# Down weights in column halves, and a scalar engine whose branch and table load come before the last down copies

## The chip, the cores and the metric

The kernel runs on one core of one Trainium2 chip. The metric is the device time of one execution in microseconds (us). The core has a tensor engine (PE, with its weight loads in rows of their own, PEld), a vector engine (DVE), a scalar engine (ACT), GpSimd (POOL) and a sync engine (SP) that issues nearly all transfers. Each engine runs its own list of instructions in order, and they wait for each other through semaphores.

## The reference

The program is one step of a one-layer decoder for 264 token rows: 256 prompt tokens (16 meta tokens go ahead of them) and 8 decoding sequences. After a mixer (a recurrent branch and a windowed attention) comes a mixture of 32 experts, of which each token takes four, and then a final norm:

```python
logits = (t @ w_router + b_router)
top_v, top_i = lax.top_k(logits, TOP_K)          # 4 of 32 experts a token
...
z = xb @ w_up[e] + b_up[e]                       # 1024 -> 2048
x_glu = jnp.minimum(z[:, ::2], SWIGLU_LIMIT)
x_lin = jnp.clip(z[:, 1::2], -SWIGLU_LIMIT, SWIGLU_LIMIT)
y = x_glu * jax.nn.sigmoid(SWIGLU_ALPHA * x_glu) * (x_lin + 1.0)
return y @ w_down[e] + b_down[e]                 # 1024 -> 1024
...
xp = xp + moe(rmsnorm(xp, norm_ffn), ...)
y_prompt = rmsnorm(xp, norm_final)[:, N_META:]
```

All weights are float32. The experts alone have 32 x (1024 x 2048 + 1024 x 1024) of them, 403 MB, and every one is read once.

## The kernel before

The first 240 us or so are the mixer and the router. Then the experts are computed in 16 pairs (`PAIRS`), two experts side by side, with up to 64 tokens each (`CAP`; a flag says whether an expert has more, and then further rounds run inside an `If`; with this data they do not). A pair's weights come in 12 loads of 2 MB (`PAIR_LOADS`): 8 of `w_up`, 4 of `w_down`. They go through a ring of 8 slots. SP issues each load as soon as the tensor engine has released a slot (semaphore `ring_used`, one count a load). The very last load is issued as two halves of 1 MB, and the second has a semaphore of its own (`half_full`).

For a pair `q` the tensor engine does, in order: the up projection into banks 0 to 3; in between, the combination of the pair before (`combine`, five units, each one 128 x 512 block of the token rows: unit 0 is rows 0 to 127 and columns 0 to 511, unit 1 the same rows and columns 512 to 1023, units 2 and 3 the next 128 rows, unit 4 the tail with both halves); the gather of the next pair's tokens; the transposition of the gated rows `y_e` (`y_rows`, in two halves); and the down projection into banks 4 and 5 (line 1174), bank 4 for output columns 0 to 511 and bank 5 for 512 to 1023. ACT copies the transposed rows to `y_t` (`yt_copy`, line 709, semaphore `yt_ready`) and the two down banks to `yd` (`yd_copy`, line 681, semaphore `yd_ready`). DVE does the gating and adds the combined units to the tokens.

Each of the four down loads of a pair holds two of the eight blocks of 128 rows of `w_down`, and all 1024 columns. So every load feeds both banks, and both banks are complete only with the last load: bank 4 after the first half of it (`down_done`), bank 5 after the second (`ring_used`).

The last pair is different. `y_rows(q, 1)` comes after its first down load, six matmuls without use (`keep_warm`) stand ahead of its down projection, and the five combinations follow the down projection in the order 0, 2, 4, 1, 3 (`LAST_ORDER`), each into a bank of its own. ACT, after its last `yd_copy`, reads the flag (line 739), branches past the `If`, loads the table of the square root with a call on one element (line 748), and goes on to the final norm: a `Square` with a row sum over each 512 columns (line 752, `square`), and three square roots (lines 761, 763, 766), for token rows 0 to 127, for the tail and for rows 128 to 255. DVE adds the units (line 1657), multiplies the first column halves by the norm weights (line 1662), takes the three reciprocals (line 1675) in the order 0, tail, 1 and scales the second column halves (line 1679). ACT scales the first halves (line 770). SP sends the second halves and the tail out (lines 424 to 430), ACT the first halves (line 773).

## Time and profile before

| | |
|---|---|
| median of three runs | 1169.79 us |
| lowest, highest | 1169.16, 1172.5 us |
| the profiled execution | 1169.19 us |
| its span in the trace | 1167.3 us |
| tensor engine busy | 1108.0 us (95%) |
| vector, scalar engine busy | 307.7 us (26%), 228.3 us (20%) |
| mean rate from and to memory over the span | 376 GB/s |

The profile records one execution. Its times are counted from the start of the span, and the span is 1.89 us shorter than the time of the same execution. A busy share is an average over stages with different limits; the rows further down are taken from the stages that matter. The times of matmuls are modelled at their ends, and matmuls overlap, so a group's span is read from its row and not from count times duration.

### The profile page before, as it was taken

The numbers are of one execution on the slowest core, as the hardware profiler recorded it, in microseconds if no ns is written. First come the engines' busy times: TensorE is split into PE (matmuls) and PEld (weight loads), VectorE is DVE, ScalarE is ACT, GpSimd is POOL, SyncE is SP. The second block draws the span as 40 slices with busy tenths as digits, with TensorE's granted clock in tenths as the row PEclk, the third lists the DMA queues.
The fourth block names the chain that finished last, engine by engine and source line by source line (L and its number), as shares of the span: only waits on it lengthen the run. The fifth ranks groups of instructions, "written<-read, shape, count | busy, mean of one in ns | idle before, by whom it ended". The sixth has DMA issues, their size and how long they took to land.

```text
span 1167.3 us, 15067 instructions
## 1 busy us (share of the span) xinstructions
PE 1108.0 (95%) x5796; PEld 501.5 (43%) x5796; DVE 307.7 (26%) x765; ACT 228.3 (20%) x641; POOL 34.0 (3%) x69
## 2 busy tenths in 40 slices
PE   9999999989999999999999898989898999999997
PEld 6687778844343434333332323232333333323322
DVE  6465553032031221313130303030303121203022
ACT  3554363331020202011010101010101010110102
POOL 0200012220000000000000000000000000000000
PEclk9999999999999999999999999999999999999999
DMA  9643637679999999999999999999999999999995
GB/s 359 233 161 108 185 110 289 288 278 411 426 427 429 428 426 427 429 427 428 428 427 429 428 427 429 429 428 428 429 427 429 428 427 429 428 426 428 428 427 202
DMA packets 39375, 438.63 MB, mean 376 GB/s; under 512 B 6576, under 2 KB 8896, under 8 KB 10416
## 3 DMA queue, kind: packets, MB, share of 16 engines
q1 hardware_dynamic: 38568, 436.17, 89.8%
q10 hardware_dynamic: 768, 1.94, 0.4%
q8 instruction: 25, 0.41, 0.1%
q14 instruction: 14, 0.11, 0.0%
HBM read 436.79 MB, written 2.41 MB: 376 GB/s over the span
## 4 chain that ended last, share of the span: by engine, by line
PE 60%; DMA 33%; ACT 3%; DVE 3%; issue 1%; SPq 0%; POOL 0%; ACTq 0%; POOLq 0%
DMA ring<-in_w_up 29%; PE bank L1128 19%; PE bank L1174 15%; PE bank L927 8%; PE bank L972 5%; PE bank L1053 3%; DMA ring<-in_w_down 3%; PE bank L1075 2%; PE bank L1086 1%; ACT area L699 1%; PE bank L1028 1%; DMA ring<-in_w_in 1%; PE bank L1050 1%; PE bank L812 1%; PE bank L1078 0%
## 5 line engine op out<-in xcount | busy, mean ns | idle before, releaser
L1128 PE MATMUL bank<-ring,area 128*64 128x512 f32 x2032 | 462.0, 599 | 30.2 <-DMA ring<-in_w_up 30.2
L1128 PEld LDWEIGHTS bank<-ring,area 128*64 128x64 f32 x2032 | 136.9, 137 | 340.0 <-issue 252.6
L1174 PE MATMUL bank<-ring,area 128*64 128x512 f32 x1008 | 220.4, 594 | 0.5 <-DMA ring<-in_w_down 0.5
L1541 DVE TENSOR_TENSOR x_tok<-x_tok,bank 128x512 f32<-128x512 f32 x60 | 41.3, 688 | 461.9 <-PE bank L1075 461.9
L689 ACT ACTIVATE area<-area 128x256 f32<-128x256 f32 x64 | 26.5, 416 | 550.2 <-DVE area L1553 550.2
L1174 PEld LDWEIGHTS bank<-ring,area 128*64 128x64 f32 x1008 | 71.0, 137 | 141.7 <-issue 135.0
L927 PE MATMUL bank<-ring 128*128 128x264 f32 (+1 forms) x544 | 129.7, 393 | 0.8 <-DMA ring<-in_w_in 0.6
L927 PEld LDWEIGHTS bank<-ring 128*128 128x128 f32 x544 | 101.1, 190 | 24.4 <-issue 4.6
L1075 PE MATMUL bank<-area 128*128 128x512 f32 x128 | 71.5, 643 | 0.0
L681 ACT ACTIVATE area<-bank 128x512 f32<-128x512 f32 x32 | 19.1, 597 | 206.2 <-PE bank L1174 206.2
L972 PE MATMUL bank<-area,ring 128*128 128x264 f32 x256 | 58.7, 388 | 0.0
L1053 PE MATMUL bank<-area,h_tok 128*128 128x128 bf16 x768 | 53.1, 220 | 0.0
L972 PEld LDWEIGHTS bank<-area,ring 128*128 128x128 f32 x256 | 48.1, 190 | 8.0 <-issue 0.2
L1053 PEld LDWEIGHTS bank<-area,h_tok 128*128 128x128 bf16 x768 | 49.5, 98 | 0.0
L1553 DVE TENSOR_SCALAR area<-bank 128x256 f32<-128x256 f32 x64 | 26.9, 420 | 76.0 <-PE bank L1128 75.9
L1075 PEld LDWEIGHTS bank<-area 128*128 128x128 f32 x128 | 19.2, 188 | 51.3 <-issue 51.3
L699 ACT ACTIVATE area<-bank,vec 128x128 f32<-128x128 f32 x120 | 34.3, 368 | 20.5 <-PE bank L1053 20.5
L1086 PE MATMUL bank<-keep,area 128*128 128x128 f32 x128 | 17.7, 280 | 13.7 <-ACT area L699 13.7
L1578 DVE TENSOR_TENSOR area<-area 128x1024 f32<-128x1024 f32 x15 | 18.4, 1225 | 40.4 <-ACT area L699 40.4
L1050 PE MATMUL bank<-area,h_tail 72*128 72x128 bf16 x128 | 28.5, 223 | 0.0
L1557 DVE SCALAR_TENSOR_TENSOR area<-area 128x256 f32<-128x256 f32 x64 | 27.2, 425 | 2.2
L1028 PE MATMUL bank<-bias_parts,chosen 96*128 96x512 bf16 x96 | 26.7, 388 | 0.5 <-ACT area L705 0.5
(252 smaller groups left out, 622.7 us busy)
## 6 DMA issues: line engine op xcount, KB each, us to landing
ring<-in_w_up SPq DMA_DIRECT2D x127, 2048.0 KB, 31.6
ring<-in_w_down SPq DMA_DIRECT2D x55, 2048.0 KB, 34.8
ring<-in_w_in SPq DMA_DIRECT2D x17, 1024.0 KB, 7.7
ring<-in_w_down SPq DMA_DIRECT2D x16, 1024.0 KB, 32.9
ring<-in_w_out SPq DMA_DIRECT2D x8, 1024.0 KB, 4.9
area<-in_w_up SPq DMA_DIRECT2D x1, 2048.0 KB, 26.8
area<-in_w_down SPq DMA_DIRECT2D x1, 2048.0 KB, 7.6
ring<-in_x_cols SPq DMA_DIRECT2D x2, 560.0 KB, 4.5
```

The source lines that it names most:

```text
L699: ins = act(xe[:, j, :], bank[6 + half][:, P * i:P * (i + 1)], ACT.Copy, scale=vec[:, NFF + j:NFF + j + 1])
L927: m = mm(proj_bank(n)[:, 0:T - lo], w[:, k, P * (n % 2):P * (n % 2) + P], (xn if n < 2 else h_t)[:, k, lo:T], start=(k == 0), stop=(k == K ...
L972: mo = mm(bank[m % 2][:, 0:NT], w[:, k, :], m_t[:, k, N_META:T], start=(k == 0), stop=(k == 2 * KB - 1))
L1028: mm(bank[b0 + n - n0][:, :], chosen[:, :], bias_parts[:, NB * n:NB * (n + 1)], start=True, stop=False, skip_group_check=True)
L1050: mm(out, h_tail[0:TRIO, P * j:P * (j + 1)], g_oh[0:TRIO, 2, :], start=True, stop=False)
L1053: m = mm(out, parts[:, t, i, P * j:P * (j + 1)], g_oh[:, t, :], start=False, stop=(t == 1 and i == 2))
L1075: m = mm(b[:, :], gw_t[:, lo:lo + P], yd[:, NB * c:NB * (c + 1)], start=True, stop=True)
L1086: tr = eng.transpose(bank[6 + half][:, P * i:P * (i + 1)], y_e[:, P * (4 * half + i):P * (4 * half + i + 1)], ident)
L1128: m = mm(bank[2 * h + n][64 * e:64 * e + 64, :], xe[:, k, 64 * e:64 * e + 64], w[:, kk, e, NB * n:NB * (n + 1)], start=False, stop=(k == K ...
L1174: m = mm(bank[4 + c][64 * e:64 * e + 64, :], y_t[:, f, 64 * e:64 * e + 64], w[:, c, e, j, :], start=False, stop=(f == KB - 1), skip_group_ ...
L1541: eng.tensor_tensor(x, x, combined_bank(unit, last)[:, :], ALU.add).then_inc(s.added, 1)
L1557: eng.scalar_tensor_tensor(out=lin[:, n % 2, :], in0=lin[:, n % 2, :], scalar=1.0, in1=glu[:, n % 2, :], op0=ALU.add, op1=ALU.mult).then_i ...
```

## The change

Three things change. First, the host packs `w_down` differently and the tensor engine reads it so: a load holds four blocks of rows and one half of the output columns. Loads 0 and 1 complete bank 4, loads 2 and 3 complete bank 5. In the last pair, `combine(q, 0)` follows load 1, and the others follow load 3. Both `yd_copy` calls now wait for `ring_used`. Second, in ACT's program `yd_copy` of the last pair moves behind the reading of the flag and the `If`, and the call that loads the square root's table moves ahead of the flag; a first `square` stands between the two last copies. Third, the square root and the reciprocal of the tail come last, the half sums come earlier, and the stores follow that order; ACT issues each of its two stores right behind the scaling that it belongs to.

The lists of the two compiled programs show what stands where. Scalar engine, end of the program before; `area` is the working memory (here `yd`), `bank` a PSUM bank:

```order
L689 ACTIVATE area<-area 128x256 [waits y_ready,glu_ready] x2
L709 ACTIVATE area<-bank 128x512 [waits ytr_done]
L681 ACTIVATE area<-bank 128x512 [waits down_done,combine_done]
L681 ACTIVATE area<-bank 128x512 [waits ring_used]
L739 TENSOR_LOAD flag
L739 ISA x2
```

and, past the `If`:

```order
L748 ACT_TABLE_LOAD
L748 ACTIVATE stat<-eps 128x1
L752 ACTIVATE area,stat<-x_tok 128x512 [waits final_added] x2
L752 ACTIVATE area,stat<-x_tail 72x512 [waits final_added]
L752 ACTIVATE area,stat<-x_tok 128x512 [waits final_added]
L761 ACTIVATE stat<-stat 128x1 [waits squares,sumsq]
L763 ACTIVATE stat<-stat,eps 72x1 [waits sumsq]
L752 ACTIVATE area,stat<-x_tok 128x512 [waits final_added]
```

Scalar engine, the same places of the changed program (its lines 678, 706, 743, 759 and 771 are lines 681, 709, 748, 752 and 761 of before):

```order
L686 ACTIVATE area<-area 128x256 [waits y_ready,glu_ready] x2
L706 ACTIVATE area<-bank 128x512 [waits ytr_done]
L743 ACT_TABLE_LOAD
L743 ACTIVATE stat<-eps 128x1
L744 TENSOR_LOAD flag
L744 ISA x2
```

and, past the `If`:

```order
L678 ACT_TABLE_LOAD [waits ring_used]
L678 ACTIVATE area<-bank 128x512 [waits combine_done]
L759 ACTIVATE area,stat<-x_tok 128x512 [waits final_added]
L678 ACTIVATE area<-bank 128x512 [waits ring_used]
L759 ACTIVATE area,stat<-x_tok 128x512 [waits final_added]
L759 ACTIVATE area,stat<-x_tail 72x512 [waits final_added]
L759 ACTIVATE area,stat<-x_tok 128x512 [waits final_added]
L771 ACT_TABLE_LOAD [waits squares]
L771 ACTIVATE stat<-stat 128x1 [waits sumsq]
L759 ACTIVATE area,stat<-x_tok 128x512 [waits final_added]
```

The last two copies of the down banks moved behind the branch. One table load stood there, ahead of everything; now three stand in the program: one ahead of the branch, one at the first copy behind it and one at the first square root.

Tensor engine, the down projection of the last pair and what follows it, before:

```order
L1174 MATMUL bank<-ring,area 64x512 [waits ring_full6,yt_ready]
L1174 MATMUL bank<-ring,area 64x512 x7
L1086 MATMUL bank<-keep,area 128x128 [waits y_ready]
L1086 MATMUL bank<-keep,area 128x128 x3
L1174 MATMUL bank<-ring,area 64x512 [waits ring_full7]
L1174 MATMUL bank<-ring,area 64x512 x7
L1174 MATMUL bank<-ring,area 64x512 [waits ring_full0,yt_ready]
L1174 MATMUL bank<-ring,area 64x512 x7
L1174 MATMUL bank<-ring,area 64x512 [waits ring_full1]
```

and changed (lines 1180, 1093 and 1082 are 1174, 1086 and 1075 of before):

```order
L1180 MATMUL bank<-ring,area 64x512 [waits ring_full6,yt_ready]
L1180 MATMUL bank<-ring,area 64x512 x7
L1093 MATMUL bank<-keep,area 128x128 [waits y_ready]
L1093 MATMUL bank<-keep,area 128x128 x3
L1180 MATMUL bank<-ring,area 64x512 [waits ring_full7,yt_ready]
L1180 MATMUL bank<-ring,area 64x512 x7
L1082 MATMUL bank<-area 128x512 [waits yd_ready,gwt_ready]
L1180 MATMUL bank<-ring,area 64x512 [waits ring_full0]
L1180 MATMUL bank<-ring,area 64x512 x7
L1180 MATMUL bank<-ring,area 64x512 [waits ring_full1]
```

The second wait for `yt_ready` moved from the third load to the second, and `combine(q, 0)`, with its wait for the copied bank, now stands between the second load and the third.

The diff:

```diff
--- before.py
+++ after.py
@@ -144,7 +144,7 @@
 x_biased x_negmax x_sink_exp x_exp x_scaled ga_sig attn_gated wout_used final_added x2_ready
 split_copy split_sub h2_tr logits_done negtop top_exp selb_ready rank_done flag_ready cast_ready gather_oh weight_oh
 gather_done xt_ready up_done glu_ready lin_ready sig_ready gated_ready y_ready ytr_done yt_ready gwt_tr
-gwt_ready down_done yd_ready combine_done added ring_used window_stored 
+gwt_ready yd_ready combine_done added ring_used window_stored 
 y_final stored router_step lru_step x_step
 """.split()
 
@@ -423,11 +423,11 @@
             eng.wait_ge(s.y_final, 3)
             eng.dma_start(y_prompt[0, 0:P, NB:D], h_tok[:, 0, NB:D]).then_inc(s.stored, 16)
             eng.wait_ge(s.y_final, 4)
+            eng.dma_start(y_prompt[0, P:2 * P, NB:D], h_tok[:, 1, NB:D]).then_inc(s.stored, 16)
+            eng.wait_ge(s.y_final, 5)
             for half in range(2):
                 eng.dma_start(y_sample[:, 0, NB * half:NB * (half + 1)], h_tok[64 * half:64 * half + B_S, 2, 0:NB])\
                    .then_inc(s.stored, 16)
-            eng.wait_ge(s.y_final, 5)
-            eng.dma_start(y_prompt[0, P:2 * P, NB:D], h_tok[:, 1, NB:D]).then_inc(s.stored, 16)
 
             eng.wait_ge(s.stored, 16 * (5 + 6))
             eng.wait_ge(s.window_stored, 16 * 10)
@@ -670,15 +670,12 @@
                 act(ex[0:n, t, :], lg[0:n, t, 0:E_N], ACT.Exp, bias=ntop[0:n, t:t + 1]).then_inc(s.top_exp, 1)
 
 
-            def yd_copy(q):
-
-                eng.wait_ge(s.combine_done, 5 * q)
-                for c in range(2):
-                    if c == 0:
-                        eng.wait_ge(s.down_done, q + 1)
-                    else:
-                        eng.wait_ge(s.ring_used, PAIR_LOADS * q + PAIR_LOADS)
-                    act(yd[:, NB * c:NB * (c + 1)], bank[4 + c][:, :], ACT.Copy).then_inc(s.yd_ready, 1)
+            def yd_copy(q, c):
+
+                if c == 0:
+                    eng.wait_ge(s.combine_done, 5 * q)
+                eng.wait_ge(s.ring_used, PAIR_LOADS * q + (UP_LOADS + 2 * c + 2))
+                act(yd[:, NB * c:NB * (c + 1)], bank[4 + c][:, :], ACT.Copy).then_inc(s.yd_ready, 1)
 
             def sigmoid(q, n):
                 eng.wait_ge(s.glu_ready, 4 * q + (n + 1))
@@ -726,49 +723,59 @@
                     gwt_copy(q)
                     yt_copy(q, 0)
                 yt_copy(q, 1)
-                yd_copy(q)
 
             rrow_copy(0)
+            def yd_copies(q):
+                yd_copy(q, 0)
+                yd_copy(q, 1)
+
             pair(0, True)
+            yd_copies(0)
             pair(1, True)
+            yd_copies(1)
             with eng.Fori(1, PAIRS // 2 - 1) as it:
-                pair(2 * it, True)
-                pair(2 * it + 1, True)
+                for u in range(2):
+                    pair(2 * it + u, True)
+                    yd_copies(2 * it + u)
             pair(PAIRS - 2, True)
+            yd_copies(PAIRS - 2)
             pair(PAIRS - 1, False, True)
+            act(stat[:, 14:15], eps[:, :], ACT.Sqrt)
             more = eng.value_load(flag[0:1, 0:1], min_val=0, max_val=1)
             with eng.If(more > 0):
                 with eng.Fori(PAIRS // 2, PAIRS // 2 * ROUNDS) as it:
                     for u in range(2):
+                        yd_copies(2 * it + u - 1)
                         rrow_copy(2 * it + u)
                         xe_copy(2 * it + u, 0)
                         xe_copy(2 * it + u, 1)
                         pair(2 * it + u, False)
 
-            act(stat[:, 14:15], eps[:, :], ACT.Sqrt)
+                eng.wait_ge(s.combine_done, 5 * (PAIRS * ROUNDS - 1))
+                eng.wait_ge(s.ring_used, PAIR_LOADS * PAIRS * ROUNDS)
 
             def square(step, x, n, col):
                 eng.wait_ge(s.final_added, step + 1)
                 act(junk[0:n, NB * step:NB * (step + 1)], x, ACT.Square, accum_out=stat[0:n, col:col + 1])\
                     .then_inc(s.squares, 1)
 
+            yd_copy(PAIRS - 1, 0)
             square(0, x_tok[:, 0, 0:NB], P, 0)
+            yd_copy(PAIRS - 1, 1)
             square(1, x_tok[:, 1, 0:NB], P, 1)
             square(2, x_tail[0:TRIO, :], TRIO, 2)
-            square(3, x_tok[:, 0, NB:D], P, 3)
-            eng.wait_ge(s.sumsq, 2)
-            eng.wait_ge(s.squares, 3 * KB + 4)
-            act(stat[:, 6:7], stat[:, 3:4], ACT.Sqrt, bias=stat[:, 5:6], scale=1.0 / D).then_inc(s.root, 1)
+            for t in range(2):
+                square(3 + t, x_tok[:, t, NB:D], P, 3 + t)
+                eng.wait_ge(s.sumsq, 2 + t)
+                eng.wait_ge(s.squares, 3 * KB + 4 + t)
+                act(stat[:, 6 + t:7 + t], stat[:, 3 + t:4 + t], ACT.Sqrt, bias=stat[:, (5, 15)[t]:(6, 16)[t]],
+                    scale=1.0 / D).then_inc(s.root, 1)
             eng.wait_ge(s.sumsq, 6)
             act(stat[0:TRIO, 8:9], stat[0:TRIO, 2:3], ACT.Sqrt, bias=eps[0:TRIO, :], scale=1.0 / D).then_inc(s.root, 1)
-            square(4, x_tok[:, 1, NB:D], P, 4)
-            eng.wait_ge(s.squares, 3 * KB + 5)
-            act(stat[:, 7:8], stat[:, 4:5], ACT.Sqrt, bias=stat[:, 15:16], scale=1.0 / D).then_inc(s.root, 1)
             for t in range(2):
                 eng.wait_ge(s.y_final, t + 1)
-                eng.wait_ge(s.rstd_ready, 2 * t + 2)
+                eng.wait_ge(s.rstd_ready, t + 2)
                 act(h_tok[:, t, 0:NB], h_tok[:, t, 0:NB], ACT.Copy, scale=stat[:, 9 + t:10 + t]).then_inc(s.y_scaled, 1)
-            for t in range(2):
                 eng.wait_ge(s.y_scaled, t + 1)
                 eng.dma_start(y_prompt[0, P * t:P * (t + 1), 0:NB], h_tok[:, t, 0:NB]).then_inc(s.stored, 16)
 
@@ -1161,24 +1168,22 @@
                 biases(4, 6, 4)
                 if last:
                     keep_warm(6, bank[0])
-                for fp in range(KB // 2):
-                    if fp % 2 == 0:
-                        eng.wait_ge(s.yt_ready, 2 * q + (fp // 2 + 1))
-                    w = full(u, UP_LOADS + fp, it).rearrange("p (c e j n) -> p c e j n", c=2, e=2, j=2)
-                    for c in range(2):
-                        if u == 1 and fp == KB // 2 - 1 and c == 1:
+                for i in range(4):
+                    c, half = divmod(i, 2)
+                    if c == 0:
+                        eng.wait_ge(s.yt_ready, 2 * q + (half + 1))
+                    w = full(u, UP_LOADS + i, it).rearrange("p (f e n) -> p f e n", f=4, e=2)
+                    for f in range(4):
+                        if u == 1 and i == 3 and f == 2:
                             eng.wait_ge(s.half_full, 16 * it + 16)
-                        for j in range(2):
-                            for e in range(2):
-                                f = 2 * fp + j
-                                m = mm(bank[4 + c][64 * e:64 * e + 64, :], y_t[:, f, 64 * e:64 * e + 64],
-                                       w[:, c, e, j, :], start=False, stop=(f == KB - 1), skip_group_check=True)
-                                if j == 1 and c == 1 and e == 1:
-                                    m.then_inc(s.ring_used, 1)
-                                elif f == KB - 1 and e == 1:
-                                    m.then_inc(s.down_done, 1)
-                    if last and fp == 0:
+                        for e in range(2):
+                            m = mm(bank[4 + c][64 * e:64 * e + 64, :], y_t[:, 4 * half + f, 64 * e:64 * e + 64],
+                                   w[:, f, e, :], start=False, stop=(half == 1 and f == 3), skip_group_check=True)
+                    m.then_inc(s.ring_used, 1)
+                    if last and i == 0:
                         y_rows(q, 1)
+                    elif last and i == 1:
+                        combine(q, 0, True)
 
             pair(0, 0, 0, 0, True, first=True)
             pair(1, 1, 0, 1, True)
@@ -1188,7 +1193,7 @@
             pair(PAIRS - 2, 0, PAIRS // 2 - 1, PAIRS - 2, True)
             pair(PAIRS - 1, 1, PAIRS // 2 - 1, PAIRS - 1, True, last=True)
 
-            for unit in LAST_ORDER:
+            for unit in LAST_ORDER[1:]:
                 combine(PAIRS - 1, unit, True)
 
             eng.wait_ge(s.flag_ready, 1)
@@ -1656,10 +1661,10 @@
                 x = x_tok[:, t, cols] if unit < 4 else x_tail[:, :]
                 eng.tensor_tensor(x, x, combined_bank(unit, True)[:, :], ALU.add).then_inc(s.final_added, 1)
                 if step < 2:
-                    if step == 1:
-                        half_sum(0)
                     eng.wait_ge(s.final_added, step + 1)
                     eng.tensor_tensor(h_tok[:, t, cols], x, norm_b[:, cols], ALU.mult).then_inc(s.y_final, 1)
+                    if step == 0:
+                        half_sum(0)
                 elif step == 2:
                     half_sum(1)
                 elif step == 3:
@@ -1669,11 +1674,11 @@
                     eng.wait_ge(s.sumsq, 5)
                     eng.tensor_tensor(stat[0:TRIO, 2:3], stat[0:TRIO, 2:3], rr[0:TRIO, 0:1], ALU.add).then_inc(s.sumsq, 1)
 
-            for step, t in enumerate((0, 2, 1)):
+            for t in range(3):
                 n = height[t]
-                eng.wait_ge(s.root, step + 3)
+                eng.wait_ge(s.root, t + 3)
                 eng.reciprocal(stat[0:n, 9 + t:10 + t], stat[0:n, 6 + t:7 + t]).then_inc(s.rstd_ready, 1)
-                eng.wait_ge(s.rstd_ready, step + 2)
+                eng.wait_ge(s.rstd_ready, t + 2)
                 out, x, scale = ((h_tok[0:n, 2, 0:NB], x_tail[0:n, :], norm_t[0:n, :]) if t == 2
                                  else (h_tok[:, t, NB:D], x_tok[:, t, NB:D], norm_b[:, NB:D]))
                 eng.scalar_tensor_tensor(out=out, in0=x, scalar=stat[0:n, 9 + t:10 + t], in1=scale,
@@ -1703,7 +1708,7 @@
     if name == "w_up":
         return a[0].reshape(PAIRS, 2, 4, 2, P, 2, D).transpose(0, 5, 2, 4, 3, 1, 6).reshape(PAIRS, KB, P, SLOT)
     if name == "w_down":
-        return a[0].reshape(PAIRS, 2, KB // 2, 2, P, 2, NB).transpose(0, 2, 4, 5, 1, 3, 6).reshape(PAIRS, KB // 2, P, SLOT)
+        return a[0].reshape(PAIRS, 2, 2, 4, P, 2, NB).transpose(0, 5, 2, 4, 3, 1, 6).reshape(PAIRS, KB // 2, P, SLOT)
     return a
```

## Rows read from the trace of the kernel before

**Rows 1.** The page: rate of the transfers in 40 equal slices of the span.

```profile
GB/s 359 233 161 108 185 110 289 288 278 411 426 427 429 428 426 427 429 427 428 428 427 429 428 427 429 429 428 428 429 427 429 428 427 429 428 426 428 428 427 202
```

**Rows 2.** Chain that ended last, near its end: start, duration, what.

```profile
1111.63 35.62 DMA ring<-in_w_down
...
1147.39 7.10 PE bank L1174 x32
```

**Rows 3.** Stretches: length, busy time by engine, clock, DMA share, GB/s.

```profile
1151.50:1154.50 3.00, 3.00 (x15) 0.93 (x11) 0.00 (x0) 0.60 (x1) 0.00 (x0) 1.00 0.00 0
```

**Rows 4.** Timeline, last down projection on PE and ACT: start, duration, what.

```profile
1143.26 3.65 PE L1174 MATMUL bank<-ring,area 128*64 128x512 f32 x16
1143.36 0.60 ACT L709 ACTIVATE area<-bank 128x512 f32<-128x512 f32 x1 [5.57 <-PE bank L1086]
...
1154.40 1.98 PE L1075 MATMUL bank<-area 128*128 128x512 f32 x4
1154.51 0.60 ACT L681 ACTIVATE area<-bank 128x512 f32<-128x512 f32 x1 [1.06 <-PE bank L1174]
...
1155.81 1.28 ACT L748 ACT_TABLE_LOAD   x1 [0.70 <-issue]
...
1157.11 0.20 ACT L748 ACTIVATE stat<-eps 128x1 f32<-128x1 f32 x1
```

**Rows 5.** Timeline, the same places of the pair before the last but one.

```profile
1022.80 1.09 ACT L709 ACTIVATE area<-bank 128x512 f32<-128x512 f32 x2 [0.54 <-PE bank L1086]
...
1023.56 13.95 PE L1174 MATMUL bank<-ring,area 128*64 128x512 f32 x64
```

**Rows 6.** Timeline of DVE, ACT and PE after the last down projection.

```profile
1155.67 0.69 DVE L1657 TENSOR_TENSOR x_tok<-x_tok,bank 128x512 f32<-128x512 f32 x1 [17.23 <-PE bank L1075]
...
1156.32 1.08 PE L1078 MATMUL bank<-area 128*64 128x512 f32 x4
...
1157.33 1.99 PE L1075 MATMUL bank<-area 128*128 128x512 f32 x4
...
1158.62 0.68 DVE L1657 TENSOR_TENSOR x_tail<-x_tail,bank 128x512 f32<-128x512 f32 x1
...
1159.34 0.63 ACT L752 ACTIVATE area<-x_tail 72x512 f32<-72x512 f32 x1 [0.80 <-DVE x_tail L1657]
...
1160.09 0.14 DVE L1667 COPY rr<-stat 8x1 f32<-8x1 f32 x1
...
1160.52 0.68 DVE L1657 TENSOR_TENSOR x_tok<-x_tok,bank 128x512 f32<-128x512 f32 x1
...
1160.81 0.29 ACT L761 ACTIVATE stat<-stat 128x1 f32<-128x1 f32 x1
1161.23 0.63 ACT L752 ACTIVATE area<-x_tok 128x512 f32<-128x512 f32 x1
...
1161.99 0.29 ACT L766 ACTIVATE stat<-stat 128x1 f32<-128x1 f32 x1
```

**Rows 7.** The same timeline, last scaling and two of the stores.

```profile
1162.12 0.37 SPq L424 DMA_DIRECT2D out_y_prompt<-h_tok  x1
...
1163.11 0.72 ACT L770 ACTIVATE h_tok<-h_tok,stat 128x512 f32<-128x512 f32 x1 [0.21 <-DVE stat L1675]
...
1163.83 0.36 SPq L430 DMA_DIRECT2D out_y_prompt<-h_tok  x1
```

**Rows 8.** Stretches of the stores, columns as in rows 3.

```profile
1162.50:1163.00 0.50, 0.00 (x0) 0.00 (x0) 0.50 (x2) 0.40 (x1) 0.00 (x0) 1.00 0.07 25
1163.50:1166.25 2.75, 0.00 (x0) 0.00 (x0) 0.30 (x1) 0.33 (x1) 0.00 (x0) 0.51 0.90 315
```

**Rows 9.** Timeline, tensor engine behind two waits for a load.

```profile
1013.49 3.65 PE L1128 MATMUL bank<-ring,area 128*64 128x512 f32 x16 [1.24 <-DMA ring<-in_w_up]
...
1044.21 5.28 PE L1128 MATMUL bank<-ring,area 128*64 128x512 f32 x16 [2.14 <-DMA ring<-in_w_up]
```

**Rows 10.** The stretch behind the longer wait, columns as in rows 3.

```profile
1044.20:1047.60 3.40, 3.39 (x8) 1.01 (x10) 0.00 (x0) 0.00 (x0) 0.00 (x0) 0.51 0.99 419
```

## The prediction, written before the changed kernel had run

> **What bounds the kernel now.** I first read the page's rates by slice [rows 1]: from the tenth slice to the last but one the core moves 411 to 429 GB/s without a dip, although the tensor engine is busy all the while. For most of the program the stream of expert weights sets the pace. The chain of waits says the same near the end [rows 2]: a down load is issued at 1111.63 us, travels for 35.62 us behind the loads before it, and on landing releases 32 matmuls. Then I read the stretches [rows 3]: from 1151.5 us on nothing is moved at all. So the stream ends there, and what follows, some 16 us, is a chain of dependent work. Nothing in the change touches the number, size or order of the weight transfers, so I expect everything up to about 1143 us where it is, and the question is only the tail. I read that from the timeline: the reader should see PE without a gap from 1147.39 to 1159.3 us [rows 2, 4, 6], and behind it DVE and ACT handing small work to each other.
>
> **The steady state.** A down load still releases its slot after eight matmuls. The second load now needs the second half of `y_t`, where before the third did. In a pair inside the loop both copies are done at 1022.80 + 1.09 = 1023.89 us, and the second load starts a quarter into the 13.95 us that begin at 1023.56, at about 1027.0 [rows 5]. The work on the first load hides the wait with 3 us to spare, so it costs nothing. The earlier copy of bank 4 meets an idle ACT and nobody asks for it before the next pair. Zero for the 15 pairs.
>
> **The second load of the last pair.** Here `y_rows(q, 1)` stands behind the first load. Before, the second load started at 1143.26 us and the copy of the transposed half ran beside it, from 1143.36 for 0.60 us [rows 4]. Now the second load waits for that copy: 1143.36 + 0.60 + 0.05 = 1144.01, which is 0.75 later. It takes 3.65 and ends at 1147.66.
>
> **The combination ahead of the third load.** PE works through its list in order. `combine(q, 0)` now stands ahead of the third load and waits for the copy of bank 4. That copy starts when the second load ends, and the list of ACT shows that a table load stands ahead of it and carries the wait for `ring_used`. So the load isn't hidden in ACT's idle time: 1147.69 + 1.28 + 0.02, copy 0.60, and PE gets its bank at 1149.64. Both durations are rows [rows 4]. PE idles for 1.98 us. The unit itself takes 0.96 (two in the 1.92 from 1154.40 to 1156.32 [rows 4, 6]) to 1.05; I take 1.0. The third load starts at 1150.65, where it started at 1147.39 [rows 2]. Everything has landed by 1151.5, so the 16 + 16 matmuls run through as before in 7.01 us (1147.39 to 1154.40) and the next unit starts at 1157.66, that is **+3.26**.
>
> **Four units instead of five.** Unit 2 needs only bank 4's copy, and unit 4 gets bank 5's during it (copy of 0.60). 0.96 + 1.01 later, at 1159.63, units 1 and 3 start, before at 1157.33 [rows 6]: the unit taken out is worth **-0.96**, and the difference is +2.30.
>
> **DVE.** A unit's add starts 1.27 us after the unit (1154.40 to 1155.67 [rows 4, 6]). Before, DVE was late for unit 1, since it had to do four adds and products first. Now one add and product are done early. The tail's add comes at about 1160.25, and unit 1's at 1160.92, bound by PE, where it was at 1159.29 (0.67 behind the tail's add at 1158.62, a step I keep). That gives back **-0.67**: +1.63.
>
> **The second table load.** `square` starts 0.72 after the add (1158.62 to 1159.34), the root 0.76 after the square (1161.23 to 1161.99) [rows 6]. So the third-last square starts at 1161.64, and at 1162.40 comes what was not there: the list shows a table load between it and the first root, **+1.28** and 0.02. The root runs at 1163.70, before at 1160.81: +2.89. The load is there because ACT can reach this place from the `If` with another table in place; the load ahead of the branch is therefore not enough, and the first copy behind the branch asks for one table and the root for another. The last square follows at 1163.92, the last of the two prompt roots at 1164.68, before at 1161.99: the tail's root, now last, gives back **-0.20**, +2.69.
>
> **What is removed.** The read of the flag and the branch (0.70 idle) and a table load (1.28) stood behind the last copy [rows 4]. They held back only the first square, which has DVE's work beside it. Now they run in ACT's idle time before 1147.66: 1143.96 + 1.28 + 0.20 + about 0.8 is 1146.2. That is free, but what it frees wasn't the end of the chain: units 4, 1 and 3 on PE ran until 1159.32 anyway.
>
> **The stores.** From 1164.68 ACT does the tail's root (0.20), the first scaling (0.70), an issue (0.36), the second scaling (0.72) and an issue (0.36), which with the small gaps ends at 1167.30; before, the last issue began at 1163.83 and ended at 1164.19 [rows 7]. That is +0.4 over the shift. In return only one store is late. A store issued at 1162.12 was seen moving only around 1163.0 [rows 7, 8], and before three of them had to go at once, at 315 GB/s until 1166.25, with 1.05 from there to the end of the span at 1167.3. Now the last 256 KB start at 1166.94 + 0.85 and take 0.83 at that rate, or up to 1.3 behind the store ahead: 1168.6 to 1169.1, and with 1.05 the span ends at 1169.7 to 1170.2. I take 1170.0.
>
> **The sum.** +3.26 - 0.96 - 0.67 + 1.28 - 0.20 is +2.71 at the roots, and the stores leave it: span 1167.3 + 2.7 = 1170.0. The same execution took 1.89 more than its span, so 1171.9. The profiled execution (1169.19) lies 0.6 under the median, and another may lie either side; I say 1172.2, which is +2.4 us or 0.2%. About 0.3%, 3.5 us, is what a measurement of this kernel can tell from no change, so this falls within it, on the slow side.
>
> **Bounds of what no row shows.** The table load that carries a wait: if it started before its wait were met, its 1.28 would be hidden, PE's gap would be 0.7 and the time 1170.7 to 1170.9; at the other end it costs all of its 1.28, as the only one in the tail did. I take the full cost, since the list is explicit. The order of banks in the matmuls changes (16 records to one bank in place of 8): the loads with the old order take 3.65 for 16 in every stage, and I take the same; nothing else in the rows bears on it.
>
> **Rivals.**
> *The clock falls in the new gap* (slower by over 0.3%). PE waited 1.24 us for a load once a pair, and the 16 matmuls behind it took 3.65 as always; once it waited 2.14, and they took 5.28 [rows 9], with a granted clock of 0.51, that is 1.2 GHz, over the following 3.4 us [rows 10]. My gap of 1.98 lies between the two and near the longer. If the clock falls there, the matmuls of the third load take 1.63 longer, and since all weights have landed nothing absorbs it: 1173.6 to 1173.9, +0.33% to +0.35%. It decides from the point at which a gap is long enough, somewhere from 1.24 to 2.14; whether it falls may differ between executions. Chance 0.38.
> *The first table load is hidden* (above): 1170.8, chance 0.10.
> *The stream covers it* (the side of faster). If the third load landed only at about 1150.6, the combination would use time that PE waits anyway. The end of the down projection would not move: 1171.9 - 3.26 = 1168.7, a gain of 0.1%. Rows 2 and 3 speak against it: it landed at 1147.25 and all was quiet at 1151.5. Chance 0.04. Even with the second table load gone as well (-1.28) that is 1167.4; a gain of 3.5 us is in no case, and I leave 0.04 for what the trace doesn't show.
> *A table switch costs more than its row.* ACT's row of the load is 1.28, and the next ACTIVATE starts 0.02 behind its end, at 1157.11 [rows 4]. If something of the same size stood beside each of the two loads on the path, the time would be 1171.9 + 2.6 = 1174.5. Chance 0.03. The Trainium skill says this: "ScalarE: Activation LUTs", section "What ACT_TABLE_LOAD costs", gives about 1283 ns for the load, which the trace confirms, and some 1380 ns more for a drain with every change of set, which the row here does not show; by it the sum would be about 1174.7.
>
> **Chances and range.** The forecast as worked out has 0.41, the clock 0.38, the hidden load 0.10, the drain 0.03, covered 0.04, unknown gain 0.04. My sum may be off by 0.7 us, so a part of the first case lands beyond 3.5 us and a part of the clock's case below it. Slower by over 0.3%: 0.44. Within 0.3%: 0.51. Faster: 0.05. The likeliest case alone spans 1171.2 to 1173.2. The range goes down to the hidden load, 1170.2, and up to the clock's case with its error, 1174.8.
>
> **What would show it.** Right: a gap of about 2 us on PE ahead of the first combination, filled by a table load and a copy on ACT; the last four units starting around 1157.7; a table load of 1.28 between the last squares and the first root, at about 1162.4; weights still all landed by 1151.5. Wrong: a PE gap of 0.7 or less; the third load's matmuls in 5.3 us; no load at the root; or any difference before 1143 us, in the rate of the stream above all.

## The result and the profile after

The changed kernel took 1174.41 us (median of 9 runs, 1172.18 to 1177.21), the kernel before 1169.75 us (9 runs, 1168.91 to 1172.5). The ratio is 1.0040, with a 95% interval of 1.0031 to 1.0048: slower by 4.7 us, or 0.4%, and clear of noise. That is within the stated range. It is not the case that I called likeliest (1172.2, within 0.3% of no change) but the one that I gave 0.38, in which the clock falls in the new gap.

The execution that was profiled took 1176.95 us, with a span of 1175.2. It began its last down projection 2.90 us later than the one before, at 1141.98 us in place of 1139.08, for a reason that has nothing to do with the tail (below). Times in the tail are therefore compared from that start on. The timeline of the changed kernel, PE and ACT in the last down projection, with start, duration and what, and in brackets the idle time before and its releaser, answers to [rows 4]:

```profile
1141.98 3.65 PE L1180 MATMUL bank<-ring,area 128*64 128x512 f32 x16
...
1146.26 0.60 ACT L706 ACTIVATE area<-bank 128x512 f32<-128x512 f32 x1 [5.57 <-PE bank L1093]
1146.88 1.28 ACT L743 ACT_TABLE_LOAD   x1
1146.91 3.66 PE L1180 MATMUL bank<-ring,area 128*64 128x512 f32 x16 [0.69 <-ACT area L706]
...
1150.66 1.28 ACT L678 ACT_TABLE_LOAD   x1 [2.29 <-PE bank L1180]
1151.96 0.60 ACT L678 ACTIVATE area<-bank 128x512 f32<-128x512 f32 x1
1152.70 1.10 PE L1082 MATMUL bank<-area 128*128 128x512 f32 x2 [2.13 <-ACT area L678]
1153.72 8.78 PE L1180 MATMUL bank<-ring,area 128*64 128x512 f32 x32
...
1162.44 1.13 PE L1082 MATMUL bank<-area 128*128 128x512 f32 x2
```

The reader should see the chain of the prediction step by step: the second load waits 0.69 for the copy of `y_t`; when it ends, ACT loads a table (1.28), only then copies (0.60), and PE has stood still for 2.13 us when it takes up the combination. The 32 records behind it take 8.78 us, where they took 7.10 [rows 2]. The stretches show why (length, busy time of PE, PEld, DVE, ACT and POOL, clock, DMA share, GB/s):

```profile
1150.60:1152.70 2.10, 0.00 (x1) 0.03 (x1) 0.00 (x0) 1.88 (x2) 0.00 (x0) 1.00 0.79 324
1152.70:1154.30 1.60, 1.60 (x4) 0.46 (x6) 0.37 (x1) 0.00 (x0) 0.00 (x0) 0.90 0.30 123
1154.30:1157.70 3.40, 3.40 (x12) 1.06 (x10) 1.16 (x3) 0.72 (x2) 0.00 (x0) 0.55 0.01 2
1157.70:1162.40 4.70, 4.70 (x24) 1.36 (x20) 0.00 (x0) 0.00 (x0) 0.00 (x0) 1.00 0.01 3
```

The fall comes a little over 1 us behind the gap: over the first 1.6 us the granted clock is 0.90, then PE worked for 3.4 us at a granted 0.55, nearly all at 1.2 GHz, and then at 2.4 GHz again. By 1154.30, which is 1151.40 in the times of before, the weights have landed, as forecast. The end of the program, answering to [rows 6, 7]:

```profile
1165.67 0.69 DVE L1662 TENSOR_TENSOR x_tok<-x_tok,bank 128x512 f32<-128x512 f32 x1
...
1167.19 1.28 ACT L771 ACT_TABLE_LOAD   x1
1168.48 0.29 ACT L771 ACTIVATE stat<-stat 128x1 f32<-128x1 f32 x1
...
1169.48 0.29 ACT L771 ACTIVATE stat<-stat 128x1 f32<-128x1 f32 x1
...
1170.61 0.36 ACTq L780 DMA_DIRECT2D out_y_prompt<-h_tok  x1
...
1171.07 0.72 ACT L778 ACTIVATE h_tok<-h_tok,stat 128x512 f32<-128x512 f32 x1 [0.49 <-DVE stat L1680]
...
1171.82 0.34 ACTq L780 DMA_DIRECT2D out_y_prompt<-h_tok  x1
```

The second table load stands between the last square but one and the first root, as the list of instructions said. At the very end an issue of 0.36 stands between the two scalings.

Counted from the first down load, each milestone of before and after (the last column is the difference):

| from the first down load, us | before | after | shift |
|---|---|---|---|
| second load starts | 4.18 | 4.93 | +0.75 |
| third load starts | 8.31 | 11.74 | +3.43 |
| next unit after the down projection | 15.32 | 20.46 | +5.14 |
| DVE adds unit 1 | 20.21 | 23.69 | +3.48 |
| first root | 21.73 | 26.50 | +4.77 |
| last root of the prompt rows | 22.91 | 27.50 | +4.59 |
| ACT's last issue of a store ends | 25.13 | 30.18 | +5.05 |
| end of the span | 28.22 | 33.22 | +5.00 |

### The profile page after: what moved, and what is told of

The parts are those of the page before. It is cut to its first block, busy times and chain, and to the rows that moved or that the text cites. A ratio compares the mean times of both kernels' runs of the same rounds, so it can differ in the third digit from the quotient of the medians.

```text
span 1175.2 us, 15074 instructions
## 1 busy us (share of the span) xinstructions
PE 1110.0 (94%) x5794; PEld 503.1 (43%) x5796; DVE 308.1 (26%) x765; ACT 230.8 (20%) x643; POOL 33.9 (3%) x69
## 3 DMA queue, kind: packets, MB, share of 16 engines
q10 hardware_dynamic: 768, 1.94, 0.5%
## 4 chain that ended last, share of the span: by engine, by line
PE 63%; DMA 30%; ACT 4%; DVE 2%; issue 1%; SPq 0%; POOL 0%; ACTq 0%; POOLq 0%
DMA ring<-in_w_up 29%; PE bank L1180 19%; PE bank L1135 17%; PE bank L934 8%; PE bank L979 5%; PE bank L1060 4%; PE bank L1082 2%; PE bank L1093 1%; ACT area L696 1%; PE bank L1035 1%; PE bank L1057 1%; DMA ring<-in_w_in 1%; PE bank L819 1%; PE bank L1045 0%; PE bank L810 0%
```

## The experiments

Each kernel was timed in five rounds against the kernel before. Beside each median stands the ratio with its 95% interval. "Last root" is the last prompt root, counted from the first down load in the profiled execution; it is 22.91 before the change and 27.50 after it. The kernel before, timed beside each group, had medians of 1169.56 to 1169.86.

**The combination behind the last load.** `combine(q, 0)` goes back behind the last load, and with it ACT's two copies stand side by side; both table loads are kept:

```diff
             yd_copy(PAIRS - 1, 0)
+            yd_copy(PAIRS - 1, 1)
             square(0, x_tok[:, 0, 0:NB], P, 0)
-            yd_copy(PAIRS - 1, 1)
...
-                    elif last and i == 1:
-                        combine(q, 0, True)
...
-            for unit in LAST_ORDER[1:]:
+            for unit in LAST_ORDER:
```

> The changed kernel with combine(q, 0) moved back behind the last down load, and ACT's two last copies next to each other ahead of the first square (otherwise the square would wait for a unit that comes later). Both table loads stay. Theory (the gap of 2.1 us in front of the first combination costs 3.3 us of the tensor engine's order and the lower clock 1.7 us on top): no gap, the third load's matmuls start 0.3 us later than before the change and take 3.6 us each at full clock; the first table load is hidden, the second stays on the path with 1.28 us; time 1171.0 +- 0.7. Rival (the place of the combination does not matter, the two table loads make all the difference): 1173.5 or more.

Measured: 1171.22 us, ratio 1.0014 (1.0005 to 1.0023), last root at 23.97, +1.06. The timeline shows 48 records in one piece and the first table load beside them:

```profile
1143.71 10.52 PE L1180 MATMUL bank<-ring,area 128*64 128x512 f32 x48 [0.69 <-ACT area L706]
...
1147.47 1.28 ACT L678 ACT_TABLE_LOAD   x1 [2.29 <-PE bank L1180]
...
1160.46 1.28 ACT L771 ACT_TABLE_LOAD   x1
```

With the combination in its old place 3.2 us of the 4.7 are gone. The table loads alone cannot be the cause of these, since both are still there; the first one costs only where PE stands behind it.

**Work without use in the gap.** The gap stays as long as it is, but PE is busy in it:

```diff
                     elif last and i == 1:
+                        keep_warm(8, bank[1])
                         combine(q, 0, True)
```

> The changed kernel with eight matmuls without use (128x512, bf16, into bank 1, some 1.7 to 2.1 us) in the gap in front of the first combination. Theory (the granted clock falls because of the gap): the clock stays at 1.0 through the third and fourth down load, the 32 records take 7.1 us in place of 8.8, the unit starts where it did or 0.1 later; time 1172.7 +- 0.6, and the spread between runs shrinks. Rival (the clock falls for another reason, or costs nothing that counts): 1174.4 as the changed kernel, or more by the added matmuls.

Measured: 1172.66 us, ratio 1.0023 (1.0014 to 1.0032), runs from 1171.99 to 1173.82, last root at 25.80. The unit starts as late as ever, and the matmuls behind it run at full clock, as the stretch shows:

```profile
1147.31 1.91 PE L790 MATMUL bank<-ones 128*128 128x512 bf16 x8
...
1149.51 1.10 PE L1082 MATMUL bank<-area 128*128 128x512 f32 x2 [0.29 <-ACT area L678]
1150.54 7.09 PE L1180 MATMUL bank<-ring,area 128*64 128x512 f32 x32
```

```profile
1150.60:1157.50 6.90, 6.90 (x33) 2.14 (x32) 1.53 (x3) 0.72 (x2) 0.00 (x0) 1.00 0.03 10
```

So 1.75 us of the changed kernel's time is the clock, bought back by useless matmuls (1.70 at the last root), and the gap itself still costs its length.

**No table load behind the branch.** One square root on one element more, at the end of the `If`:

```diff
                 eng.wait_ge(s.ring_used, PAIR_LOADS * PAIRS * ROUNDS)
+                act(stat[:, 14:15], eps[:, :], ACT.Sqrt)
```

> The changed kernel with one more square root on one element at the end of the branch that is not taken. Then the square root's table is in place on both ways, and the compiled list has neither the table load at the first copy nor the one at the first root. Theory: the gap on the tensor engine is 0.7 us in place of 2.1, the clock stays, 1.28 off at the gap, 1.65 off for the clock, 1.28 off at the root: 1170.2 +- 0.6. Rival (the table loads run beside other waits, only the combination's place costs): 1173 or more.

Measured: 1170.64 us, ratio 1.0009 (1.0000 to 1.0018), last root at 23.40. One call at the end of a branch that this data never takes removes both loads, because then the root's table is in place whichever way ACT comes. The gap shrinks to 0.85, the clock stays, and 3.8 us come back. These overlap with the 3.2 of the late combination, since 1.28 of the gap and the fall of the clock need both, the early combination and the load ahead of its copy:

```profile
1147.77 0.60 ACT L678 ACTIVATE area<-bank 128x512 f32<-128x512 f32 x1 [2.31 <-PE bank L1181]
1148.51 1.10 PE L1083 MATMUL bank<-area 128*128 128x512 f32 x2 [0.85 <-ACT area L678]
1149.54 7.09 PE L1181 MATMUL bank<-ring,area 128*64 128x512 f32 x32
```

**Only the first of the two loads hidden.**

```diff
+            act(junk[:, 3000:3001], eps[:, :], ACT.Copy)
             yd_copy(PAIRS - 1, 0)
```

> The changed kernel with a copy of one element right behind the branch, so that the first of the two table loads runs in ACT's idle time and only the one at the first root stays. Theory: gap 0.7 us, full clock, 1.28 at the root still there: 1171.5 +- 0.6, that is 1.3 above the kernel with neither load. Rival (the load at the root is hidden behind DVE, the first one is all that counts): the same as the kernel with neither, 1170.2.

Measured: 1171.25 us, ratio 1.0017 (1.0008 to 1.0026), last root at 24.52, +1.12 against the kernel with neither load. In time it is 0.6 above that kernel, with intervals that overlap. In the profile the load at the root is on the path: the first root comes 1.27 later and the last 1.12. The missing part of the time may lie in the stores, for in the trace of the kernel with neither load the span ends 6.43 behind the last root, in this one 5.55; why is open.

```profile
1145.33 1.28 ACT L762 ACT_TABLE_LOAD   x1
...
1147.62 0.60 ACT L678 ACTIVATE area<-bank 128x512 f32<-128x512 f32 x1 [0.80 <-PE bank L1181]
...
1161.15 1.28 ACT L772 ACT_TABLE_LOAD   x1
1162.45 0.29 ACT L772 ACTIVATE stat<-stat 128x1 f32<-128x1 f32 x1
```

**Both edits together**, the late combination and no table load behind the branch:

> Both of the former edits: combine(q, 0) behind the last down load, and no table load behind the branch. Theory (the parts add): the kernel with the late combination, 1171.2, less the 1.28 of the load at the root: 1169.9 +- 0.5, the kernel before within noise. Rival (with one cause gone the other is hidden): 1171 or more.

Measured: 1170.40 us, ratio 1.0004 (0.9995 to 1.0013), last root at 22.93. The load at the root is worth 1.04 at the last root here (23.97 to 22.93) and 1.27 at the first. The median is 0.5 above what I expected and cannot be told from the kernel before. Beside the kernel without loads but with the early combination (23.40) the last root comes only 0.47 earlier: without the load ahead of its copy, the early combination costs half a microsecond and not three.

**Each half of the change alone.** First the weights in column halves with the early combination, and the other engines' programs of before but for the semaphore that the copies wait for (against the kernel before):

```diff
-                yd_copy(q)
+                yd_copy(q, 0)
+                yd_copy(q, 1)
...
+                for i in range(4):
+                    c, half = divmod(i, 2)
...
+                    elif last and i == 1:
+                        combine(q, 0, True)
...
-            for unit in LAST_ORDER:
+            for unit in LAST_ORDER[1:]:
```

> Only the column halves of the down weights and the combination ahead of the third load; ACT's, DVE's and SP's programs are those of the kernel before (both copies ahead of the branch, one table load behind it). Theory: no table load at the first copy, so the gap is 0.85 and the clock stays; the third load starts at 1149.5 in place of 1147.4, the last four units end 1.1 later than the five of before; the branch and the table load now hold all squares back, since the last copy is 2 later: 1171.0 +- 0.7. Rival (the weight layout itself is slower or faster in the 15 pairs): a difference at 1139 us already, time outside 1170.3 to 1171.7.

Measured: 1171.81 us, ratio 1.0019 (1.0010 to 1.0028), last root at 25.07. That is 0.8 above what I expected, just outside my bounds. The gap was 0.85 and the clock full. Here the branch and the load do count:

```profile
1159.32 1.28 ACT L746 ACT_TABLE_LOAD   x1 [0.70 <-issue]
...
1160.72 0.61 ACT L750 ACTIVATE area<-x_tok 128x512 f32<-128x512 f32 x1
...
1161.46 0.15 DVE L1644 TENSOR_SCALAR stat<-stat 128x1 f32<-128x1 f32 x1 [1.71 <-ACT area L750]
```

Then ACT's, DVE's and SP's new order without table loads behind the branch, with the weights and matmuls of before (against the changed kernel):

```diff
+                    eng.wait_ge(s.down_done, q + 1)
...
+                act(stat[:, 14:15], eps[:, :], ACT.Sqrt)
...
-                for i in range(4):
-                    c, half = divmod(i, 2)
...
+                for fp in range(KB // 2):
```

> Only the other half: weights, matmuls and combinations of the kernel before, with the branch ahead of the last copies, the new order of squares, roots, reciprocals and stores, and no table load behind the branch. Theory: the branch and the table load of before held back only the first square, and the tensor engine's five units and DVE's adds set the end, so their removal gives 0 to 0.6: 1169.2 to 1169.8. Rival (they were on the path with all of their 2.2 us): 1167.6 to 1168.0.

Measured: 1170.22 us, ratio 1.0007 (0.9998 to 1.0016), last root at 22.86, that is 0.05 earlier than before. Moving the branch and the table load off the path behind the last copy was worth 0.05 us at the root, and not 2.2: the rival falls. The time is 0.4 above the upper end of what I expected. Its trace shows part of it behind the root, in the stores: the span ends 5.51 behind the last root, before 5.31. The rest of the 0.45 above the kernel before can't be told from noise.

**Interleaved loads.** Bank 4 is complete with the third load, `combine(q, 0)` stands in the middle of the fourth. No table load stands behind the branch, and ACT's two copies stand side by side:

```diff
-                    c, half = divmod(i, 2)
+                    half, c = divmod(i, 2)
...
+                        if last and i == 3 and f == 1:
+                            combine(q, 0, True)
```

> Down loads in the order rows 0-3 columns 0, rows 0-3 columns 1, rows 4-7 columns 0, rows 4-7 columns 1: bank 4 is complete with the third load and is copied beside the fourth; combine(q, 0) stands in the middle of the fourth load, where its copy is ready; no table load behind the branch. Theory: no gap anywhere, neither for y_t nor for the copy; the tensor engine's work ends where it did before, DVE has a unit less to do at the end (it was 0.7 late for unit 1): 1168.8 to 1169.4, the first that is not slower than the kernel before. Rival (DVE's and ACT's chain sets the end whatever the tensor engine's order): 1169.8, the same as the kernel before.

Measured: 1170.34 us, ratio 1.0001 (0.9992 to 1.0010), last root at 22.67. No gap for `y_t` nor for the copy, but the expectation was missed: the ratio shows no gain, the median lies above the rival's 1169.8, and the last root comes 0.24 earlier than before the change, where DVE's unit less should have given 0.7. I had left the first square behind the second copy, and DVE waited 1.60 us for it. The square moved ahead of the copy again:

> The kernel with interleaved down loads, with the first square of ACT ahead of the copy of bank 5 again. In that kernel's trace the first half sum of DVE waited 1.6 us for this square, which stood behind the copy, and held the next add back until 1.43 us behind the start of its unit (1.27 elsewhere). Theory: the half sum is done beside the matmuls, the last root comes 0.2 to 0.3 earlier: 1169.9 to 1170.2, and no different from the kernel before within what can be told. Rival (DVE's late start at the end of that kernel is what ate the expected gain of a unit): 1169.3 or less.

Measured: 1169.73 us, ratio 1.0001 (0.9991 to 1.0010), last root at 22.42; on another chip once more:

> The same kernel with the stores in between, again, on the same chip for the comparison. Theory: 1169.7 +- 0.4, 0.3 to 0.6 above its neighbour. Rival: no difference between the two.

Measured: 1169.69 us, ratio 1.0004 (0.9995 to 1.0013). The last root now comes 0.49 earlier than before the change (22.42 in both traces), and the kernel is as fast as before. DVE's wait for the square explains 0.25 of what was missing. The stores were left. In the next kernel ACT issues both behind both scalings:

```diff
                 act(h_tok[:, t, 0:NB], h_tok[:, t, 0:NB], ACT.Copy, scale=stat[:, 9 + t:10 + t]).then_inc(s.y_scaled, 1)
+            for t in range(2):
                 eng.wait_ge(s.y_scaled, t + 1)
```

> The kernel with interleaved down loads and the first square ahead of the copy of bank 5, with ACT's two stores issued behind both scalings, as before the change. Theory (the new order of scaling, issue, scaling, issue costs ACT some 0.5 us at the very end, since the issue stands between the scalings, and nothing gives it back: with the last prompt root 0.5 earlier than before the change that kernel was still no faster): 1169.2, 0.5 less than with the stores in between, at the edge of what can be told; in the trace the last issue ends 2.2 after the last prompt root in place of 2.7. Rival (two stores at once queue on the DMA engines and the end stays): the last issue 0.5 earlier, the end of the span not, 1169.7.

Measured: 1169.22 us, ratio 0.9999 (0.9990 to 1.0008), against 1169.69 for its neighbour. Its two scalings run into one another, and ACT's last issue ends 2.08 us after the last root:

```profile
1162.50 0.29 ACT L772 ACTIVATE stat<-stat 128x1 f32<-128x1 f32 x1
...
1162.89 1.32 ACT L779 ACTIVATE h_tok<-h_tok,stat 128x512 f32<-128x512 f32 x2
...
1163.63 0.95 ACTq L782 DMA_DIRECT2D out_y_prompt<-h_tok  x2
```

In its neighbour that was 2.68 (root at 1162.61, last issue from 1164.95 for 0.34). From the last root to the end of the span it is 5.40 and 5.59, so of the 0.60 only 0.19 arrives: the last issue of all is SP's for the tail, which ends 2.82 and 2.83 after the last root in the two. The difference in time is 0.47 with intervals that overlap: the trace shows it, the times only suggest it. No kernel of this study beats the kernel before by more than can be told.

**The changed kernel again**, unchanged, to see how the clock's fall spreads over runs:

> The changed kernel again, unchanged, beside the runs of the kernel before on the same chip. Theory (the clock falls in the gap in most executions but not in all): median 1173.8 to 1174.8, with single runs near 1172.2 where the mean granted clock of the run is higher by the share of one 3.4 us stretch. Rival (the clock always falls): no run under 1173.2.

Measured: 1174.70 us (five runs: 1172.27, 1174.16, 1174.70, 1174.80, 1174.98), ratio 1.0040 (1.0026 to 1.0053). Its trace has the same gap of 2.13, and the fall of the clock comes earlier, in the combination itself:

```profile
1150.85 1.26 PE L1082 MATMUL bank<-area 128*128 128x512 f32 x2 [2.13 <-ACT area L678]
1152.04 8.57 PE L1180 MATMUL bank<-ring,area 128*64 128x512 f32 x32
```

One run of the five (1172.27), and one of the first nine (1172.18), lie 2.2 us or more under the median. Both had a mean granted clock of 0.997 over the run, where the others had 0.992 to 0.994; a stretch of 3.4 us at half rate is 0.0015 of that mean. So they had fewer of these stretches. That one of them was the one in the gap fits the times, 1172.2 and 1172.3, but no trace of these two runs shows it.

## Why the prediction was right, and where it was off

*The steady state, zero.* Right. Up to the first down load of the last pair nothing differs that the change could have caused: with the same clock up to there (last section), kernels with the old layout and with the new one begin it at 1139.08 and 1139.07 us alike (before; no load behind the branch).

*The second load, +0.75.* Measured +0.75.

*The combination ahead of the third load, +3.26.* Measured +3.43. The table load did carry the wait and cost its 1.28 in full; I had allowed 0.05 from the end of the copy to PE's start, and the rows show 0.14. Without this step 3.2 us are gone from the median, and without the table load in it (and at the root) 3.8: the step costs what it does because the load stands in it.

*One unit less, -0.96; DVE not late, -0.67.* From the end of the down projection to the start of the last two units the shift went from +5.14 to +4.27, that is -0.87, and DVE's add gave back another 0.79. Both near what I had.

*The second table load, +1.28.* Measured +1.29 at the first root in the changed kernel. Between kernels with and without it, it is 1.27 at the first root in both pairs, and 1.04 and 1.12 at the last. The tail's root, for which I had -0.20, gave back 0.18.

*The stores, 0.* This term was mis-sized, though the 0.4 in it was seen. I had the issue between the scalings cost 0.4 and be given back by a shorter queue. It is not given back: from the last root to the end of the span it is 5.72 us, and 5.31 before the change. So +0.41 in place of 0. The other kernels show that this is the order of the stores: 5.30 in the other trace with the old order, 5.51 to 5.65 in nine traces with the new one (and 6.43 once, open). Only 0.19 of it is the issue between the scalings, which the kernel with both of ACT's stores behind both scalings takes out (5.40 in place of 5.59).

*The first table load hidden* (a rival) falls by the row: it starts when the second load ends. *The stream covers it* falls: with the late combination PE takes up the third load without a wait some 8.5 us behind the first, here only at 11.74. *A switch of tables costs more than its row* falls: ACT's copy started 0.02 behind the load, and the root 0.01. The Trainium skill ("ScalarE: Activation LUTs", section "What ACT_TABLE_LOAD costs") adds a drain of some 1380 ns to the load at every switch to another set. Neither of these loads shows one, and the measurement decides: the gap of 2.13 is filled by the load's 1.28, the copy's 0.60 and small steps, and without the load at the root the first root came 1.27 earlier.

*The choice of the case.* This is where the prediction was off. I had two ends for the gap, 1.24 without a fall and 2.14 with one [rows 9], and put my 1.98 on the side of no fall, though it was far nearer to the other end. The gap was 2.13, and the clock fell in both traces taken. With the fall my own sum gave 1173.6 to 1173.9, and with the 0.41 of the stores 1174.0 to 1174.3; the median is 1174.41. Of my signs of being wrong one came, the slow matmuls of the third load. So the mechanism of every step but the stores was right, and the central number was low by the clock: the range held the result because this rival was priced. The useless matmuls in the gap settle that it is the clock: 1.75 us less with nothing else changed. That 0.3% is what can be told from no change was too wide: the interval here is 0.09% to either side.

## What to carry to other kernels

Work that is moved forward in an in-order engine's list brings its wait with it, and everything behind it waits too. Before moving a unit ahead of a load, add up the chain that makes its input, on whatever engine, and put the unit where that chain is already done: in the middle of the last load, with the loads interleaved, it cost no gap; one load earlier it cost a gap of 0.85 with the copy alone in the chain, and of 2.13 with the table load too.

A table loaded ahead of a branch is only kept if the branch that is not taken also ends with it. Look for the loads in the compiled list and not in the source: one call in dead code was worth 3.8 us here.

A gap costs its length, and the matmuls behind it may cost nearly as much again through the clock (1.75 here). A copy or load taken out of a gap can be worth twice its duration, if the gap becomes short enough for the clock to stay: 0.85 did not make it fall, 2.13 did. What lies between is read from the fourteen traces of this study. Leaving out the waits of 4.2 us and the start of the program, PE waited 0.80 to 1.75 us more than 400 times, and the clock never fell. It waited 1.94 to 2.45 us 19 times, and the clock fell 16 times: always from 2.12 on, and in five of the eight cases from 1.94 to 2.06. The same wait can go either way, as it does here in the same place of two kernels (no load behind the branch; the changed kernel again), with 16 matmuls in 3.65 or in 5.35 us:

```profile
1044.18 3.65 PE L1136 MATMUL bank<-ring,area 128*64 128x512 f32 x16 [2.04 <-DMA ring<-in_w_up]
```

```profile
1045.15 5.35 PE L1135 MATMUL bank<-ring,area 128*64 128x512 f32 x16 [2.04 <-DMA ring<-in_w_up]
```

So a planned gap of some 2 us should be priced with the fall as the likelier case.

## What the runs showed of the hardware that I had not expected

The clock of the tensor engine goes with most of the difference between the profiled executions up to the tail. After a wait of 4.2 us for the router, at about 241 us, every trace has one stretch at the lower level, of 3.4 us in five of the fourteen and 6.8 in nine (worked out from the clock over 10 us: 0.83 is 3.4 us at half rate, 0.66 is 6.8). The stretches around it, before, with no load behind the branch, and with interleaved loads:

```profile
240.00:250.00 10.00, 8.97 (x86) 6.13 (x88) 4.57 (x21) 4.37 (x9) 2.70 (x11) 0.83 0.58 210
```

```profile
240.00:250.00 10.00, 8.90 (x86) 6.04 (x88) 4.66 (x22) 4.45 (x9) 2.79 (x11) 0.83 0.58 210
```

```profile
240.00:250.00 10.00, 9.11 (x68) 5.93 (x69) 4.44 (x18) 4.28 (x8) 2.62 (x11) 0.66 0.57 210
```

With 0.83 the last down projection starts at 1139.08 and 1139.07, with 0.66 at 1140.48. The profiled execution of the changed kernel had 0.66 there and a further fall at 8 to 16 us (0.79, before 1.00), behind a wait of 2.45 us for a load, and started at 1141.98:

```profile
8.00:16.00 8.00, 6.30 (x20) 4.81 (x21) 3.60 (x4) 1.23 (x3) 0.00 (x0) 0.79 1.01 411
```

All fourteen traces fall into three such groups by the start of the last down projection, whatever their layout of the weights: 1138.79 to 1139.08 with the short stretch, 1140.07 to 1140.48 with the long one, and 1141.95 to 1142.33 with the long one and the early fall (three traces). So some 1.4 us for the first and 1.5 to 2 for the second reach the last pair, although 900 us of a stream at full rate lie in between, which did not make up the late start. A fall at 1044 us, behind a wait for a load inside the stream, costs nothing that arrives: of the five traces with the short stretch three have it and begin the last down projection at 1138.79 to 1139.08, two have not and begin it at 1138.93 and 1139.07. No run changed the early clock alone, so the grouping is shown and the cause is argued. The two profiled executions of the kernel with the square moved ahead differ by 2.1 us here (1142.33, 1140.19) without any difference in code, and a tail is better read from a milestone close ahead of it than from the start of the span.
